# An fp32 encoder block on one core: attention output with V stationary, gate chunks in quarters, conv taps one by one

## The chip, the core and the metric

One core of a Trainium2 chip. The metric is device time in microseconds of one execution of the whole kernel: the lower the better. Engines: TensorE (PE; its weight loads are PEld), VectorE (DVE), ScalarE (ACT), GpSimd (POOL), and the queue of SyncE (SP), which issues the loads.

## The reference, cut to what matters

One layer on 512 tokens of width 1024, all in fp32: a gated feed-forward, a mixer, a second feed-forward and a gated embedding. The mixer projects the normalised input `u` with `w_in` and runs two branches, an attention (MLA) and an mLSTM; the change lies in the attention part of it.

```python
c_q, c_kv, k_r, ml_q, ml_k, ml_v, ml_i, ml_f, ml_o, gates = jnp.split(u @ w_in, split_idx, axis=-1)
# attention: 8 heads, 64 + 32 features per head in q and k, 64 in v, 512 keys
s = einsum('bqhd,bkhd->bhqk', qn, k_nope) + einsum('bqhd,bkd->bhqk', qr, k_rope)
o = einsum('bhqk,bkhd->bqhd', softmax(s * scale, axis=-1), v)
# mLSTM: q, k = silu(depthwise_conv(ml_q | ml_k)), 5 taps; 2 directions, 4 chunks of 128
a, bm = mla_branch(...) @ w_branch_mla, mlstm_branch(...) @ w_branch_ml
mixed = (sigmoid(g_a) * a + sigmoid(g_b) * bm) @ w_out
```

## The kernel before, in words

Products with large weights run as three fp32r matmuls of 512 columns (`three`, L282 to L284, for features on partitions; `three_tm`, L289 to L291, for tokens on partitions): both operands are split into a high and a low part. Weights come in 512 KB chunks through a ring of four: SP loads `w_raw`, ScalarE writes `w_hi` (L305), VectorE `w_lo` (L312), TensorE uses both. `hi_upto` and `lo_upto` place these splits in the programs of ScalarE and VectorE; `GAC`, `MV`, `MO`, `GBC` number the chunks of the first gates, of `ml_v`, of `ml_o` and of the second gates. The attention and the mLSTM cores run as plain fp32 matmuls. Each engine's order is written out by hand in `mixer_pe`, `mixer_dve`, `mixer_act`, `mixer_pool`, with semaphores between them; there is no planner. `B[0]` to `B[7]` are the eight PSUM banks.

Attention goes by heads and by blocks of 128 queries, 32 blocks in all. For each block TensorE makes the scores (L884, Q stationary, 512 keys as columns, banks 2 to 4), VectorE the maximum and the bias (L1142, L1143), ScalarE the exp with its sum (L1345, into `Pm`); one head later TensorE transposes the block of P in four pieces (L892, banks 5 and 6), ScalarE (even blocks, L1348) and VectorE (odd, L1152) copy it to `PT`, and TensorE multiplies (`pv`, L870): the transposed P stationary, 64 columns of V moving, four matmuls per block into bank 7. `o_out` (L1125) scales a head's output with the reciprocal of the sums into `O`, tokens on partitions. Between heads TensorE does one whole chunk of the gates `g_a` (`fm_pair`, banks 0 and 1), and VectorE a `w_lo` split and, for heads 1 to 4, the five conv taps of one tile (`conv_tile`, L1058, L1060). `ga_out` (L1133) empties the gate banks after each second chunk. After the last head `O` is transposed in 16 pieces (L910) and split into `oT_hi` (L1353) and `oT_lo` (L1161). Then come `MV` (V of the mLSTM, L1364), `MO` (`og`, L1387) and the eight units of the mLSTM, the first of which starts with `mb(0)` (L963, L968, banks 2 and 7).

Of the kernel before, what the change touches and what calls it, by code (L numbers as in the profile page):

```python
# [22 lines left out]
ALU = mybir.AluOpType  # L23
ACT = mybir.ActivationFunctionType
# [93 lines left out]
def block_build(nc, w, const, out, ctx):  # L118
# [57 lines left out]
    O = ar("O", [P, TB, S], 64.5)  # L176
    PT = ar("PT", [P, 2, S], 72.5)
# [4 lines left out]
    oT_hi = ar("oT_hi", [P, 4, S], 16.5, F32R)  # L182
    oT_lo = ar("oT_lo", [P, 4, S], 24.5, F32R)
# [612 lines left out]

    def q_padded(hh, c):

        return (mqk if hh % 2 == 0 else tbuf)[:, hh // 2, c * P:(c + 1) * P]

    def mixer_pe(pe):
# [62 lines left out]
        def pv(t):  # L864
            hh, b = t // 4, t % 4
            pe.wait_ge(ms["pt_even"] if t % 2 == 0 else ms["pt_odd"], t // 2 + 1)
            if b == 0 and hh >= 1:
                pe.wait_ge(ms["o_done"], hh)
            for kb in range(TB):
                last = nc.tensor.matmul(B[7][:, b * VDIM:(b + 1) * VDIM], PT[:, t % 2, kb * P:(kb + 1) * P],  # L870
                                        Vm[:, kb, hh * VDIM:(hh + 1) * VDIM], start=(kb == 0), stop=(kb == TB - 1))
            last.then_inc(ms["pv"], 1)

        for hd in range(HEADS + 1):
            for b in range(TB):
                if hd < HEADS:
                    s = 4 * hd + b
                    if b == 0:
                        pe.wait_ge(ms["K_done"], hd + 1)
                    if s < 3:  # L880
                        pe.wait_ge(ms["Vm_done"], s + 2)
                    else:
                        pe.wait_ge(ms["exp"], s - 2)
                    nc.tensor.matmul(B[2 + s % 3][:], Q[:, hd, b * P:(b + 1) * P], K[:, hd, :], start=True,  # L884
                                     stop=True).then_inc(ms["scores"], 1)
                if hd >= 1:
                    t = 4 * (hd - 1) + b
                    pe.wait_ge(ms["exp"], t + 1)
                    if t >= 2:
                        pe.wait_ge(ms["pt_even"] if t % 2 == 0 else ms["pt_odd"], t // 2)  # L890
                    for kb in range(TB):
                        last = nc.tensor.transpose(B[5 + t % 2][:, kb * P:(kb + 1) * P],  # L892
                                                   Pm[:, b, kb * P:(kb + 1) * P], ident[:])
                    last.then_inc(ms["pT"], 1)
                    if t >= 1:
                        pv(t - 1)
            if hd < HEADS:
                if hd % 2 == 0 and hd >= 2:
                    pe.wait_ge(ms["ga"], hd)
                fm_pair(pe, GAC + hd, hd % 2, [0, 1], v_hi, v_lo, KD)  # L900
        pv(4 * HEADS - 1)

        MVB, MOB = [2, 3, 4, 7], [0, 1, 5, 6]
        for j in range(4):
            if j == 0:
                pe.wait_ge(ms["o_done"], HEADS)
            if j >= 2:
                pe.wait_ge(ms["oT_split"], j - 1)
            for tb in range(TB):
                last = nc.tensor.transpose(B[5 + j % 2][:, tb * P:(tb + 1) * P], O[:, tb, j * P:(j + 1) * P], ident[:])  # L910
            last.then_inc(ms["oTT"], 1)
# [27 lines left out]
        for pr in range(2):  # L939
            for c in range(TB):  # L940
                last = nc.tensor.transpose(B[4 + 3 * pr][:, c * P:(c + 1) * P], mqk[:, 2 + pr, c * P:(c + 1) * P], ident[:])
            last.then_inc(ms["kT_T"], 1)
# [29 lines left out]
        pe.wait_ge(ms["q_split"], 6)  # L972
        mb(0)
# [76 lines left out]
    def conv_tile(dve, ct):  # L1050

        o = mqk[:, ct, :]
        wc = VEC["ml_conv_w"]
        for j in range(CONV):
            sc = cols[:, wc + 4 * j + ct:wc + 4 * j + ct + 1]
            src = conv_in[:, ct, j:j + S]
            if j == 0:
                ins = nc.vector.tensor_scalar(o, src, sc, None, ALU.mult)  # L1058
            else:
                ins = nc.vector.scalar_tensor_tensor(o, src, sc, o, ALU.mult, ALU.add)  # L1060
            if j < CONV - 1:
                dlink(dve, ins)
            else:
                ins.then_inc(ms["conv_done"], 1)
# [4 lines left out]
    def mixer_dve(dve):  # L1069
# [51 lines left out]
        def o_out(hh):  # L1121
            dve.wait_ge(ms["exp"], 4 * hh + 4)
            dlink(dve, nc.vector.reciprocal(rsum, sums[:, 4 * hh:4 * hh + 4]))
            dve.wait_ge(ms["pv"], 4 * hh + 4)
            nc.vector.tensor_tensor(O[:, :, hh * VDIM:(hh + 1) * VDIM],  # L1125
                                    B[7][:, 0:4 * VDIM].rearrange("p (b v) -> p b v", b=4),
                                    rsum[:, :, None].broadcast_to([P, TB, VDIM]), ALU.mult).then_inc(ms["o_done"], 1)
            dve.wait_ge(ms["o_done"], hh + 1)

# [5 lines left out]
        for hd in range(HEADS + 1):  # L1135
            for b in range(TB):
                if hd < HEADS:
                    s = 4 * hd + b
                    dve.wait_ge(ms["scores"], s + 1)
                    if s >= 4:  # L1140
                        dve.wait_ge(ms["exp"], s - 3)
                    dlink(dve, nc.vector.tensor_reduce(mx[:, b:b + 1], B[2 + s % 3][:], AX.X, ALU.max))  # L1142
                    nc.vector.tensor_scalar(nb[:, b:b + 1], mx[:, b:b + 1], rqs[:, b:b + 1], -1.0, ALU.mult,  # L1143
                                            ALU.mult).then_inc(ms["nb"], 1)
                if hd >= 2 and b == 0:
                    o_out(hd - 2)
                if hd % 2 == 0 and hd >= 2 and b == 1:
                    ga_out(hd // 2 - 1)
                if hd >= 1 and b % 2 == 1:
                    t = 4 * (hd - 1) + b  # L1150
                    dve.wait_ge(ms["pT"], t + 1)
                    nc.vector.tensor_copy(PT[:, 1, :], B[6][:]).then_inc(ms["pt_odd"], 1)  # L1152
            if hd < HEADS:
                lo_upto(dve, GAC + hd + 3)
                if 1 <= hd <= 4:
                    conv_tile(dve, hd - 1)
        o_out(HEADS - 1)

        for j in range(4):
            dve.wait_ge(ms["oT_hi"], j + 1)  # L1160
            nc.vector.tensor_tensor(oT_lo[:, j, :], B[5 + j % 2][:], oT_hi[:, j, :].bitcast(F32),  # L1161
                                    ALU.subtract).then_inc(ms["oT_split"], 1)
# [152 lines left out]
    def mixer_act(act):  # L1315
# [21 lines left out]
        for hd in range(HEADS + 1):  # L1337
            for b in range(TB):
                t = 4 * (hd - 1) + b
                if hd >= 1:  # L1340
                    act.wait_ge(ms["pT"], t + 1)
                if hd < HEADS:
                    s = 4 * hd + b
                    act.wait_ge(ms["nb"], s + 1)
                    nc.scalar.activation(Pm[:, b, :], B[2 + s % 3][:], ACT.Exp, bias=nb[:, b:b + 1],  # L1345
                                         scale=rqs[:, b:b + 1], accum_out=sums[:, s:s + 1]).then_inc(ms["exp"], 1)
                if hd >= 1 and b % 2 == 0:
                    nc.scalar.activation(PT[:, 0, :], B[5][:], ACT.Copy).then_inc(ms["pt_even"], 1)  # L1348
            if hd < HEADS:
                hi_upto(act, GAC + hd + 3)  # L1350
        for j in range(4):
            act.wait_ge(ms["oTT"], j + 1)
            nc.scalar.activation(oT_hi[:, j, :], B[5 + j % 2][:], ACT.Copy).then_inc(ms["oT_hi"], 1)  # L1353
# [4 lines left out]
        for ct in range(4):  # L1358
            act.wait_ge(ms["conv_done"], ct + 1)
            nc.scalar.activation(mqk[:, ct, :], mqk[:, ct, :], ACT.Silu,  # L1360
                                 bias=col("ml_conv_b", ct)).then_inc(ms["mqk_done"], 1)
        act_after(act, MV + 3)
        for tb in range(TB):
            nc.scalar.activation(V[:, tb, :], B[[2, 3, 4, 7][tb]][:], ACT.Copy, scale=rc[:, tb:tb + 1]).then_inc(ms["Vml"], 1)  # L1364
# [10 lines left out]
        for pr in range(2):  # L1375
            act.wait_ge(ms["kT_T"], pr + 1)
            nc.scalar.activation(K_tm[:, :, pr * P:(pr + 1) * P], v4(B[4 + 3 * pr][:]), ACT.Copy).then_inc(ms["K_tm"], 1)
# [8 lines left out]
        for tb in range(TB):  # L1386
            nc.scalar.activation(og[:, tb, :], B[[0, 1, 5, 6][tb]][:], ACT.Copy,  # L1387
                                 scale=rc[:, tb:tb + 1]).then_inc(ms["mo"], 1)
# [477 lines left out]
```

## Time and profile before

| | us |
|---|---|
| median of 3 runs (1317.93 to 1319.42) | 1318.46 |
| profiled execution | 1314.45 |
| its span, first to last instruction | 1312.5 |
| PE busy | 1253.6 (96%) |
| PEld busy | 1033.7 (79%) |
| DVE busy | 677.8 (52%) |
| ACT busy | 425.5 (32%) |
| POOL busy | 119.0 (9%) |

Busy is the time in which at least one instruction of the engine ran. Matmuls are pipelined, so that records overlap: what a matmul costs in a row of others is read from start to start. A plain fp32 matmul stands in the trace as two records. The mean granted clock of TensorE over the span is 0.979 of 2.4 GHz.

### The profile page before, as it was taken

Reading aid. Unit: us, or ns where it says so; the run is one execution under the profiler, and the core shown is the slowest. Engines: PE = TensorE matmul, PEld = TensorE weight load, DVE = VectorE, ACT = ScalarE, POOL = GpSimd, SP = SyncE. Lnnn points to the kernel's source line nnn. Section 1 sums busy time; section 2 is a strip of 40 time slices with the busy share of each in tenths; the row PEclk is TensorE's granted clock in tenths of the full one; section 3 lists DMA queues with packets and bytes.
Section 4 is the critical chain, followed back from the end, with each engine's and each line's share of the span. In section 5 each row is a group of like instructions: output and inputs, shape, how many; then the busy total and the mean of one; then the engine's idle time right before and its main releaser. Section 6 shows DMA issues by size and latency. Waiting matters only on the chain.

```text
span 1312.5 us, 15620 instructions
## 1 busy us (share of the span) xinstructions
PE 1253.6 (96%) x5909; PEld 1033.7 (79%) x5909; DVE 677.8 (52%) x1042; ACT 425.5 (32%) x612; POOL 119.0 (9%) x96
## 2 busy tenths in 40 slices
PE   5899999999997999999999999989999999999996
PEld 4688888888876877777788878778888888888785
DVE  5744444432237766754555566485444444222774
ACT  3423333221133433335321333243323232112552
POOL 3000000000024000000200200230000000000343
PEclk8899999999998999999999999989999999999997
DMA  5233333222231231110221122213333332333101
GB/s 188 82 111 96 96 96 96 96 97 96 96 74 31 66 112 48 49 32 17 81 88 42 49 80 97 81 48 113 96 96 96 96 96 96 96 98 111 57 24 64
DMA packets 95810, 107.75 MB, mean 82 GB/s; under 512 B 15030, under 2 KB 85398, under 8 KB 95766
## 3 DMA queue, kind: packets, MB, share of 16 engines
q1 hardware_dynamic: 95766, 107.15, 26.3%
q8 instruction: 29, 0.48, 0.1%
q14 instruction: 15, 0.12, 0.0%
HBM read 105.04 MB, written 2.10 MB: 82 GB/s over the span
## 4 chain that ended last, share of the span: by engine, by line
PE 81%; DVE 9%; issue 5%; ACT 2%; POOL 2%; DMA 1%; SPq 0%; DVEq 0%; POOLq 0%; ACTq 0%
PE bank L282 23%; PE bank L284 23%; PE bank L283 23%; PE bank L870 2%; PE bank L884 2%; DVE v_lo L455 1%; PE bank L410 1%; DVE w_lo L312 1%; DVE tbuf L448 1%; PE bank L892 1%; PE bank L289 1%; PE bank L376 1%; POOL sqacc L396 1%; PE bank L290 1%; PE bank L291 1%
## 5 line engine op out<-in xcount | busy, mean ns | idle before, releaser
L312 DVE TENSOR_TENSOR w_lo<-w_raw,w_hi 128x1024 fp32r<-128x1024 f32 x195 | 241.5, 1244 | 386.9 <-ACT w_hi L305 379.5
L282 PE MATMUL bank<-v_hi,w_hi 128*128 128x512 f32 x968 | 381.4, 394 | 6.6 <-DVE w_lo L312 6.2
L284 PE MATMUL bank<-v_hi,w_lo 128*128 128x512 f32 x968 | 377.6, 390 | 0.0
L283 PE MATMUL bank<-v_lo,w_hi 128*128 128x512 f32 x968 | 377.3, 390 | 0.0
L305 ACT ACTIVATE w_hi<-w_raw 128x1024 fp32r<-128x1024 f32 x195 | 203.8, 1054 | 364.5 <-PE bank L284 361.0
L282 PEld LDWEIGHTS bank<-v_hi,w_hi 128*128 128x128 f32 x968 | 182.2, 188 | 44.6 <-DVE w_lo L312 6.5
L284 PEld LDWEIGHTS bank<-v_hi,w_lo 128*128 128x128 f32 x968 | 182.0, 188 | 38.3
L283 PEld LDWEIGHTS bank<-v_lo,w_hi 128*128 128x128 f32 x968 | 182.3, 188 | 37.7 <-issue 0.2
L284 PE MATMUL bank<-prod_hi,w_lo 128*128 (+1 forms) x352 | 137.0, 389 | 0.0
L282 PE MATMUL bank<-prod_hi,w_hi 128*128 (+1 forms) x352 | 137.0, 389 | 0.0
L283 PE MATMUL bank<-prod_lo,w_hi 128*128 (+1 forms) x352 | 137.0, 389 | 0.0
L282 PEld LDWEIGHTS bank<-prod_hi,w_hi 128*128 128x128 f32 x352 | 66.1, 188 | 13.8
L283 PEld LDWEIGHTS bank<-prod_lo,w_hi 128*128 128x128 f32 x352 | 66.1, 188 | 13.7
L284 PEld LDWEIGHTS bank<-prod_hi,w_lo 128*128 128x128 f32 x352 | 66.1, 188 | 13.7
L393 POOL COPY sqacc<-scratch 128x512 f32<-128x512 f32 x4 | 2.4, 611 | 745.8 <-ACT scratch L437 745.8
L675 ACT ACTIVATE prod_hi<-scratch 128x512 f32 (+1 forms) x44 | 27.1, 633 | 110.9 <-DVE scratch L639 110.9
L639 DVE TENSOR_TENSOR scratch<-bank,scratch 128x512 f32<-128x512 f32 x44 | 28.3, 685 | 65.6 <-PE bank L284 65.6
L486 POOL TENSOR_TENSOR sqacc<-sqacc,scratch 128x512 f32<-128x512 f32 x28 | 45.3, 1618 | 24.1 <-ACT scratch L476 24.0
L1345 ACT ACTIVATE Pm<-bank,small 128x512 f32<-128x512 f32 x32 | 24.9, 778 | 64.1 <-DVE small L1143 64.1
L669 ACT ACTIVATE scratch<-scratch 128x512 f32<-128x512 f32 x44 | 27.1, 633 | 53.6 <-DVE scratch L627 53.6
L504 PE MATMUL bank<-v_hi,w_hi 128*128 128x512 f32 x64 | 28.2, 440 | 12.0 <-ACT v_hi L473 12.0
L473 ACT ACTIVATE v_hi<-h,cols 128x512 fp32r<-128x512 f32 x32 | 23.1, 722 | 48.7 <-DVE h L449 44.3
(268 smaller groups left out, 1416.7 us busy)
## 6 DMA issues: line engine op xcount, KB each, us to landing
w_raw<-in_ffn_w_gate SPq DMA_DIRECT2D x44, 512.0 KB, 3.5
w_raw<-in_ffn_w_up SPq DMA_DIRECT2D x44, 512.0 KB, 3.5
w_raw<-in_ffn_w_down SPq DMA_DIRECT2D x44, 512.0 KB, 3.4
w_raw<-in_w_in SPq DMA_DIRECT2D x32, 512.0 KB, 3.6
w_raw<-in_w_out SPq DMA_DIRECT2D x8, 512.0 KB, 3.3
w_raw<-in_ple_w_gate SPq DMA_DIRECT2D x8, 512.0 KB, 3.3
x_tm<-in_x SPq DMA_DIRECT2D x2, 1024.0 KB, 5.1
w_raw<-in_w_branch_mla SPq DMA_DIRECT2D x4, 512.0 KB, 3.3
```

Of the source, the lines that this page charges most:

```text
L282: nc.tensor.matmul(o, whi, a_hi, start=start, stop=False)
L283: nc.tensor.matmul(o, whi, a_lo, start=False, stop=False)
L284: return nc.tensor.matmul(o, wlo, a_hi, start=False, stop=stop)
L305: nc.scalar.activation(w_hi[:, s, :], w_raw[:, s, :], ACT.Copy).then_inc(w_hi_done, 1)
L312: nc.vector.tensor_tensor(w_lo[:, s, :], w_raw[:, s, :], w_hi[:, s, :].bitcast(F32), ALU.subtract).then_inc(w_lo_done, 1)
L486: nc.gpsimd.tensor_tensor(sqacc[:], sqacc[:], scratch[:, m % 4, :], ALU.add).then_inc(b["h_acc"], 1)
L504: nc.tensor.matmul(o[:], whi, v_hi[:, k, :], start=(k == 0), stop=False)
L639: nc.vector.tensor_tensor(scratch[:, 2 + f, :], B[(6 if first else 2) + f][:], scratch[:, f, :], ALU.mult).then_inc(prod_done, 1)
L669: nc.scalar.activation(scratch[:, f, :], scratch[:, f, :], ACT.Silu).then_inc(silu0 if first else silu_done, 1)
L675: nc.scalar.activation(o, scratch[:, 2 + f, :], ACT.Copy).then_inc(phi, 1)
L870: last = nc.tensor.matmul(B[7][:, b * VDIM:(b + 1) * VDIM], PT[:, t % 2, kb * P:(kb + 1) * P], Vm[:, kb, hh * VDIM:(hh + 1) * VDIM], start ...
L884: nc.tensor.matmul(B[2 + s % 3][:], Q[:, hd, b * P:(b + 1) * P], K[:, hd, :], start=True, stop=True).then_inc(ms["scores"], 1)
```

## The change

- The output of attention is made with V stationary (128 keys x 64 features of one head) and the transposed P moving (512 queries). Head 2p goes to partitions 0 to 63 of bank 7, head 2p + 1 to 64 to 127, in turn over the four blocks of keys (`pair_output`). The result has features on partitions: `O`, its transposes and `o_out` are gone; `oT_high` and `oT_low` split bank 7 directly.
- P is scaled by the reciprocal of its sum before it is transposed: a reciprocal of one column on VectorE and one scaling pass on ScalarE per block.
- The blocks go in turn over the two heads of a pair (`head_block`). The transposed P of even blocks (head 2p) is kept in `scratch`, that of odd blocks in `PT_odd`, a whole head each.
- TensorE's steps: `scores(s)`, `p_transposes(s - 4)`, a quarter of a gate chunk (`fm_quarter`, 6 fp32r matmuls); after steps 11, 19, 27 and 35 a `pair_output`. VectorE does one conv tap per step (`conv_tap`, steps 6 to 25).
- Banks: `MV` and `MO` get others, and `mb(0)` waits for the first `og` copy, which reads bank 7. `oT_hi` and `oT_lo` lie interleaved in one tile.

The diff, cut to its core:

```diff
...
+    PT_odd = ar("PT_odd", [P, TB, S], 64.5)
...
+    oT = ar("oT", [P, 4, 2, S], 16.5, F32R)
+    oT_hi, oT_lo = oT[:, :, 0, :], oT[:, :, 1, :]
...
+    def fm_quarter(n, half, banks, kk):
+
+        for f in range(2):
+            k, c = 4 * half + kk, kk * 256 + f * P
+            last = three(B[banks[f]][:], wv(n, c, c + P), v_hi[:, k, :], v_lo[:, k, :], k == 0, k == KD - 1)
+        return last
...
+        def scores(s):
+            hd, b = head_block(s)
+            if b == 0:
+                pe.wait_ge(ms["K_done"], hd + 1)
+            if s < 3:
+                pe.wait_ge(ms["Vm_done"], s + 2)
+            else:
+                pe.wait_ge(ms["exp"], s - 2)
+            nc.tensor.matmul(B[2 + s % 3][:], Q[:, hd, b * P:(b + 1) * P], K[:, hd, :], start=True,
+                             stop=True).then_inc(ms["scores"], 1)
+        def p_transposes(t):
+            pe.wait_ge(ms["norm"], t + 1)
+            if t >= 2:
+                pe.wait_ge(ms["pt_even"] if t % 2 == 0 else ms["pt_odd"], t // 2)
             for kb in range(TB):
+                last = nc.tensor.transpose(B[5 + t % 2][:, kb * P:(kb + 1) * P],
+                                           Pm[:, t % 4, kb * P:(kb + 1) * P], ident[:])
+            last.then_inc(ms["pT"], 1)
+        def pair_output(pr):
+            pe.wait_ge(ms["pt_even"], 4 * pr + 4)
+            pe.wait_ge(ms["pt_odd"], 4 * pr + 4)
+            if pr >= 1:
+                pe.wait_ge(ms["oT_split"], pr)
+            for kb in range(TB):
+                for e in range(2):
+                    hd = 2 * pr + e
+                    last = nc.tensor.matmul(B[7][64 * e:64 * e + 64, :], Vm[:, kb, hd * VDIM:(hd + 1) * VDIM],
+                                            (scratch if e == 0 else PT_odd)[:, kb, :], start=(kb == 0),
+                                            stop=(kb == TB - 1))
             last.then_inc(ms["pv"], 1)
 
+        for s in range(STEPS + 4):
+            if s < STEPS:
+                scores(s)
+            if s >= 4:
+                p_transposes(s - 4)
+                c, kk = (s - 4) // 4, s % 4
+                if kk == 0:
+                    pe.wait_ge(w_lo_done, GAC + c + 1)
+                    if c % 2 == 0 and c >= 2:
+                        pe.wait_ge(ms["ga"], c)
+                last = fm_quarter(GAC + c, c % 2, [0, 1], kk)
+                if kk == 3:
+                    last.then_inc(w_used, 1)
+            if s >= 11 and s % 8 == 3:
+                pair_output(s // 8 - 1)
+        MVB, MOB = [5, 2, 3, 4], [7, 0, 1, 6]
...
-                last = nc.tensor.transpose(B[4 + 3 * pr][:, c * P:(c + 1) * P], mqk[:, 2 + pr, c * P:(c + 1) * P], ident[:])
+                last = nc.tensor.transpose(B[4 + pr][:, c * P:(c + 1) * P], mqk[:, 2 + pr, c * P:(c + 1) * P], ident[:])
...
+        pe.wait_ge(ms["mo"], 1)
         mb(0)
...
+    def conv_tap(dve, i):
+        ct, j = i // CONV, i % CONV
         o = mqk[:, ct, :]
+        c = VEC["ml_conv_w"] + 4 * j + ct
+        src = conv_in[:, ct, j:j + S]
+        if j == 0:
+            ins = nc.vector.tensor_scalar(o, src, cols[:, c:c + 1], None, ALU.mult)
+        else:
+            dve.wait_ge(ms["conv_tap"], i)
+            ins = nc.vector.scalar_tensor_tensor(o, src, cols[:, c:c + 1], o, ALU.mult, ALU.add)
+        ins.then_inc(ms["conv_tap"], 1)
+    STEPS = HEADS * TB
+    def head_block(s):
+        return 2 * (s // 8) + s % 2, s % 8 // 2
...
+        def oT_low(pr):
+            dve.wait_ge(ms["oT_hi"], pr + 1)
+            nc.vector.tensor_tensor(oT_lo[:, pr, :], B[7][:], oT_hi[:, pr, :].bitcast(F32),
                                     ALU.subtract).then_inc(ms["oT_split"], 1)
+        for s in range(STEPS + 4):
+            if s < STEPS:
+                b, q = head_block(s)[1], s % 4
+                dve.wait_ge(ms["scores"], s + 1)
+                if s >= 4:
+                    dve.wait_ge(ms["exp"], s - 3)
+                dlink(dve, nc.vector.tensor_reduce(mx[:, q:q + 1], B[2 + s % 3][:], AX.X, ALU.max))
+                nc.vector.tensor_scalar(nb[:, q:q + 1], mx[:, q:q + 1], rqs[:, b:b + 1], -1.0, ALU.mult,
+                                        ALU.mult).then_inc(ms["nb"], 1)
+            if 2 <= s < STEPS + 2:
+                r = s - 2
+                dve.wait_ge(ms["exp"], r + 1)
+                if r >= 4:
+                    dve.wait_ge(ms["norm"], r - 3)
+                nc.vector.reciprocal(rsum[:, r % 4:r % 4 + 1], sums[:, r:r + 1]).then_inc(ms["rsum"], 1)
+            if s in (12, 20, 28):
+                ga_out(s // 8 - 1)
+            if s >= 14 and s % 8 == 6:
+                oT_low(s // 8 - 1)
+            if s >= 4 and s % 2 == 1:
+                t = s - 4
+                dve.wait_ge(ms["pT"], t + 1)
+                nc.vector.tensor_copy(PT_odd[:, :, head_block(t)[1] * P:(head_block(t)[1] + 1) * P],
+                                      v4(B[6][:])).then_inc(ms["pt_odd"], 1)
+            if s % 4 == 1 and s >= 5:
+                lo_upto(dve, GAC + (s - 5) // 4 + 3)
+            if s >= 6 and s - 6 < 4 * CONV:
+                conv_tap(dve, s - 6)
+        ga_out(3)
+        oT_low(3)
...
+        def oT_high(pr):
+            act.wait_ge(ms["pv"], pr + 1)
+            nc.scalar.activation(oT_hi[:, pr, :], B[7][:], ACT.Copy).then_inc(ms["oT_hi"], 1)
+        for s in range(STEPS + 4):
+            t = s - 4
+            if t >= 0:
+                act.wait_ge(ms["pT"], t + 1)
+            if s < STEPS:
+                b, q = head_block(s)[1], s % 4
+                act.wait_ge(ms["nb"], s + 1)
+                nc.scalar.activation(Pm[:, q, :], B[2 + s % 3][:], ACT.Exp, bias=nb[:, q:q + 1],
+                                     scale=rqs[:, b:b + 1], accum_out=sums[:, s:s + 1]).then_inc(ms["exp"], 1)
+            if t >= 0 and t % 2 == 0:
+                bt = head_block(t)[1]
+                nc.scalar.activation(scratch[:, :, bt * P:(bt + 1) * P], v4(B[5][:]), ACT.Copy).then_inc(ms["pt_even"], 1)
+            if 2 <= s < STEPS + 2:
+                q = (s - 2) % 4
+                act.wait_ge(ms["rsum"], s - 1)
+                act.wait_ge(ms["exp"], s - 1)
+                nc.scalar.activation(Pm[:, q, :], Pm[:, q, :], ACT.Copy, scale=rsum[:, q:q + 1]).then_inc(ms["norm"], 1)
+            if s >= 14 and s % 8 == 6:
+                oT_high(s // 8 - 1)
+            if s % 4 == 0 and s >= 4:
+                hi_upto(act, GAC + (s - 4) // 4 + 3)
+        oT_high(3)
...
-            act.wait_ge(ms["conv_done"], ct + 1)
+            act.wait_ge(ms["conv_tap"], CONV * (ct + 1))
...
+            nc.scalar.activation(V[:, tb, :], B[[5, 2, 3, 4][tb]][:], ...
+            nc.scalar.activation(K_tm[...], v4(B[4 + pr][:]), ...
+            nc.scalar.activation(og[:, tb, :], B[[7, 0, 1, 6][tb]][:], ...
```

## Rows read from the trace of the kernel before

**Rows 1.** The page, part 4: the chain that ended last, by engine.

```profile
PE 81%; DVE 9%; issue 5%; ACT 2%; POOL 2%; DMA 1%; SPq 0%; DVEq 0%; POOLq 0%; ACTq 0%
```

**Rows 2.** Busy time of the attention stretch (columns: PE, PEld, DVE, ACT, POOL, PEclk, DMA share, GB/s).

```profile
487.86:611.12 123.26, 119.49 (x656) 91.38 (x655) 72.97 (x135) 46.49 (x93) 0.00 (x0) 1.00 0.13 39
```

**Rows 3.** Timeline of one head's steps (start us, duration us, engine, line, operation).

```profile
541.02 0.39 PE L284 MATMUL bank<-v_hi,w_lo 128*128 128x512 f32 x1
...
541.25 1.02 PE L884 MATMUL bank<-K,Q 128*128 128x512 f32 x2
...
542.11 0.60 PE L892 MATMUL bank<-ident,Pm 128*128 128x128 f32 x4
...
542.54 1.00 PE L870 MATMUL bank<-Vm,PT 128*128 128x64 f32 x8
...
543.38 1.08 PE L884 MATMUL bank<-K,Q 128*128 128x512 f32 x2
...
550.55 0.48 PE L282 MATMUL bank<-v_hi,w_hi 128*128 128x512 f32 x1
550.63 0.19 PEld L283 LDWEIGHTS bank<-v_lo,w_hi 128*128 128x128 f32 x1
550.87 0.39 PE L283 MATMUL bank<-v_lo,w_hi 128*128 128x512 f32 x1
```

**Rows 4.** Groups by line, 487.8 to 611.1 us: attention output on TensorE.

```profile
L870 PE MATMUL bank<-Vm,PT 128*128 128x64 f32 x256 | 34.1, 276 | 1.7 <-ACT PT L1348 0.7 <-DVE PT L1152 0.3 <-DVE O L1125 0.2
```

**Rows 5.** Timeline of TensorE at the end of the stretch.

```profile
599.74 0.39 PE L284 MATMUL bank<-v_hi,w_lo 128*128 128x512 f32 x1
...
607.95 1.09 PE L910 MATMUL bank<-ident,O 128*128 128x128 f32 x8 [0.59 <-DVE O L1125]
610.14 1.25 PE L910 MATMUL bank<-ident,O 128*128 128x128 f32 x8 [1.10 <-DVE oT_lo L1161]
611.15 0.47 PE L289 MATMUL bank<-w_hi,v_hi 128*128 128x512 f32 x1
```

**Rows 6.** Timeline of TensorE at the start of the stretch.

```profile
487.86 2.74 PE L884 MATMUL bank<-K,Q 128*128 128x512 f32 x6
490.98 1.12 PE L884 MATMUL bank<-K,Q 128*128 128x512 f32 x2 [0.39 <-ACT Pm L1345]
491.55 0.80 PE L282 MATMUL bank<-v_hi,w_hi 128*128 128x512 f32 x1
```

**Rows 7.** Groups by line, same stretch: VectorE and ScalarE (`Vm`: 476 to 490 us).

```profile
L1345 ACT ACTIVATE Pm<-bank,small 128x512 f32<-128x512 f32 x32 | 24.9, 778 | 64.1 <-DVE small L1143 64.1
L1142 DVE TENSOR_REDUCE small<-bank 128x1 f32<-128x512 f32 x32 | 22.1, 690 | 27.7 <-PE bank L884 27.2
...
L1060 DVE SCALAR_TENSOR_TENSOR mqk<-conv_in,cols,mqk 128x512 f32<-128x512 f32 x16 | 12.0, 752 | 0.6
...
L312 DVE TENSOR_TENSOR w_lo<-w_raw,w_hi 128x1024 fp32r<-128x1024 f32 x9 | 11.0, 1224 | 10.2 <-ACT w_hi L305 10.2
...
L1348 ACT ACTIVATE PT<-bank 128x512 f32<-128x512 f32 x16 | 9.4, 588 | 7.0 <-PE bank L892 7.0
...
L1143 DVE TENSOR_SCALAR small<-small 128x1 f32<-128x1 f32 x32 | 6.8, 214 | 1.1
...
L1133 DVE TENSOR_TENSOR gates_a<-bank,r_b 128x512 f32<-128x512 f32 x8 | 5.1, 681 | 0.0
...
L1123 DVE RECIPROCAL small<-small 128x4 f32<-128x4 f32 x8 | 1.3, 168 | 0.0
...
L1335 ACT ACTIVATE Vm<-bank,small 128x512 f32<-128x512 f32 x4 | 2.8, 688 | 2.8 <-PE bank L291 2.8
```

**Rows 8.** Timeline around the first `Mb` group, 655 to 664 us.

```profile
658.90 1.15 PE L963 MATMUL bank<-Mrows,ident 8*128 8x128 f32 x8
659.01 2.42 ACT L1387 ACTIVATE og<-bank,small 128x512 f32<-128x512 f32 x4 [1.93 <-PE bank L291]
...
661.48 0.50 PE L282 MATMUL bank<-v_hi,w_hi 128*128 128x512 f32 x1 [0.34 <-ACT og L1387]
```

More of the change, by code:

```diff
@@ L175, in block_build @@
     Pm = ar("Pm", [P, TB, S], 56.5)
-    O = ar("O", [P, TB, S], 64.5)
-    PT = ar("PT", [P, 2, S], 72.5)
+    PT_odd = ar("PT_odd", [P, TB, S], 64.5)
     mqk = ar("mqk", [P, 4, S], 76.5)
@@ L180, in block_build @@
     i_row = tbuf[0:8, 1, :]
-    oT_hi = ar("oT_hi", [P, 4, S], 16.5, F32R)
-    oT_lo = ar("oT_lo", [P, 4, S], 24.5, F32R)
+    oT = ar("oT", [P, 4, 2, S], 16.5, F32R)
+    oT_hi, oT_lo = oT[:, :, 0, :], oT[:, :, 1, :]
     gates_b = ar("gates_b", [P, 8, S], 32.5)
@@ L862, in mixer_pe @@
         pe.wait_ge(ms["Q_done"], HEADS)
[L864 to L868, printed above, removed]
-            for kb in range(TB):
-                last = nc.tensor.matmul(B[7][:, b * VDIM:(b + 1) * VDIM], PT[:, t % 2, kb * P:(kb + 1) * P],
-                                        Vm[:, kb, hh * VDIM:(hh + 1) * VDIM], start=(kb == 0), stop=(kb == TB - 1))
-            last.then_inc(ms["pv"], 1)
@@ L874, in mixer_pe @@
[L874 to L911, printed above, removed]
+        def scores(s):
[8 more added lines that the diff above has]
+                             stop=True).then_inc(ms["scores"], 1)
@@ L1048, in block_build @@
     UNITS = [(0, 0), (1, 3), (0, 1), (1, 2), (0, 2), (1, 1), (0, 3), (1, 0)]
-    def conv_tile(dve, ct):
+    def conv_tap(dve, i):
+        ct, j = i // CONV, i % CONV
         o = mqk[:, ct, :]
[L1053 to L1064, printed above, removed]
+        c = VEC["ml_conv_w"] + 4 * j + ct
[9 more added lines that the diff above has]
+        return 2 * (s // 8) + s % 2, s % 8 // 2
     def v4(ap):
@@ L1119, in mixer_dve @@
                                     ALU.mult).then_inc(ms["K_done"], 1)
[L1121 to L1128, printed above, removed]
         def ga_out(g):
@@ L1133, in ga_out @@
                 nc.vector.tensor_tensor(gates_a[:, 2 * g + f, :], B[f][:], r_b[:], ALU.mult).then_inc(ms["ga"], 1)
[L1135 to L1161, printed above, removed]
-                                    ALU.subtract).then_inc(ms["oT_split"], 1)
+        def oT_low(pr):
+            dve.wait_ge(ms["oT_hi"], pr + 1)
+            nc.vector.tensor_tensor(oT_lo[:, pr, :], B[7][:], oT_hi[:, pr, :].bitcast(F32),
+                                    ALU.subtract).then_inc(ms["oT_split"], 1)
@@ L1335, in mixer_act @@
             nc.scalar.activation(Vm[:, tb, :], B[VB[tb]][:], ACT.Copy, scale=rq[:, 4 + tb:5 + tb]).then_inc(ms["Vm_done"], 1)
[L1337 to L1353, printed above, removed]
+        def oT_high(pr):
[23 more added lines that the diff above has]
+        oT_high(3)
         for m in range(8):
@@ L1363, in mixer_act @@
         for tb in range(TB):
-            nc.scalar.activation(V[:, tb, :], B[[2, 3, 4, 7][tb]][:], ACT.Copy, scale=rc[:, tb:tb + 1]).then_inc(ms["Vml"], 1)
+            nc.scalar.activation(V[:, tb, :], B[[5, 2, 3, 4][tb]][:], ACT.Copy, scale=rc[:, tb:tb + 1]).then_inc(ms["Vml"], 1)
         for d in range(2):
@@ L1376, in mixer_act @@
             act.wait_ge(ms["kT_T"], pr + 1)
-            nc.scalar.activation(K_tm[:, :, pr * P:(pr + 1) * P], v4(B[4 + 3 * pr][:]), ACT.Copy).then_inc(ms["K_tm"], 1)
+            nc.scalar.activation(K_tm[:, :, pr * P:(pr + 1) * P], v4(B[4 + pr][:]), ACT.Copy).then_inc(ms["K_tm"], 1)
         act.wait_ge(ms["decb_ps"], 1)
@@ L1386, in mixer_act @@
         for tb in range(TB):
-            nc.scalar.activation(og[:, tb, :], B[[0, 1, 5, 6][tb]][:], ACT.Copy,
+            nc.scalar.activation(og[:, tb, :], B[[7, 0, 1, 6][tb]][:], ACT.Copy,
                                  scale=rc[:, tb:tb + 1]).then_inc(ms["mo"], 1)
```

## The prediction, made before the changed kernel ran

> **What bounds the kernel now.** I read the chain of waits first: 81% of the span is TensorE, 9% VectorE [rows 1]. Then the stretch that the change rewrites, from the first score matmul to the first matmul of the `MV` chunks, 487.86 to 611.15 us, 123.3 us: TensorE is busy for 119.5 us of it at a full granted clock (1.00) [rows 2]. So the stretch is worth what TensorE issues in it, plus the waits that its order makes. The timeline of one head gives the price of each kind of group, from start to start [rows 3]: after a gate matmul (541.02, next 541.25) the score matmul takes 0.86 us (541.25 to 542.11, two records, since a plain fp32 matmul is recorded as two passes), the four transposes of a block 0.43, the four attention-output matmuls of a block 0.84 (542.54 to 543.38, eight records of 64 columns). In the gate matmuls (fp32r, 512 columns) one start follows another after 0.23 us, the first after fp32 work after 0.32 (550.55 to 550.87). Attention output has 256 records in all, the largest group after the gates: 34.1 us busy [rows 4]. Last, the end of the stretch: the last gate matmul starts at 599.74, `MV` at 611.15; in these 11.4 us stand a head of output, 16 transposes of `O` and two waits for VectorE (0.59 and 1.10 us) that nothing covers [rows 5].
>
> **The change part by part.** TensorE's own work in the new order:
>
> Scores: 32 x 0.86 = 27.5 us. Transposes of P: 32 x 0.43 = 13.8 us. Both as before.
>
> Gate quarters: 32 groups of 6 fp32r matmuls. A group costs 0.32 + 5 x 0.23 = 1.46 us, since each now follows fp32 transposes: 46.6 us. Before, 8 groups of 24 cost 8 x (0.32 + 23 x 0.23) = 44.9; the cutting costs 1.7 us.
>
> Attention output: 32 matmuls of 512 columns in place of 128 of 64. One is 2 records of 0.43 us, as the score matmul, of the same columns and type [rows 3], so a pair of heads is 16 records. Here the trace of before shows no operation of the kind: nothing in it fills only half of the columns. Bounds: if the two halves never run side by side, 16 x 0.43 = 6.9 us a pair, 27.5 in all, about what the 256 short records take; if they always do, 3.4 us a pair, 13.8 in all. Below that it can't fall, each half having 8 records to stream. I take nearly full overlap. The two heads write different partitions of the bank and hold separate weights, but the order of issue is e0, e0, e1, e1: with starts in order, the first record of e1 can only go with the second of e0, so the pair takes one record more than the bound, 9 x 0.43 = 3.9 us, 15.5 us in all. The row nearest to it is the score matmul's, which can't choose between the ends: it gives the price of a record, not which records share time. I choose the overlap because each stream reads 512 columns in 0.43 us, so two at once read no faster than one fp32r stream does now (512 in 0.23 us): no rate is asked for that the trace does not show. Both ends stay in the range.
>
> The `O` transposes, their waits and the rounds through ScalarE and VectorE between them (607.95 to 611.15 [rows 5]) go. In their place `oT` is split out of bank 7 while TensorE goes on with other work: three of four in the middle of the steps; the last is needed only by `MO`, behind 96 matmuls of `MV`, 96 x 0.23 = 22 us. What is late next there is nothing.
>
> Sum of work: 27.5 + 13.8 + 46.6 + 15.5 = 103.4 us.
>
> Waits in the new order, on TensorE:
>
> 1. Gate banks 0 and 1. At steps 12, 20 and 28 the first quarter of a new pair waits for both of `ga_out`, which VectorE now issues in the same step, behind max, `nb` and reciprocal of that step's scores. VectorE needs 0.69 + 0.21 + 0.17 + 2 x 0.68 us from the end of the scores [rows 7], somewhat less where short ones follow closely, say 2.3 with the handing over; TensorE has 0.43 us of transposes to do meanwhile, and the end of a score record lies 0.17 us behind the next start. 2.1 us each, three times: 6.4. Everything behind it in TensorE's queue waits too, and so the next scores. Before, `ga_out` stood two blocks ahead of its use and no such wait shows. For this wait the bounds are 1.5 and 2.8 us.
>
> 2. The start. Before, the gates of head 0 (from 491.55) cover the first exp. Now steps 0 to 3 have only scores: the wait for exp before the fourth stays, and the first transposes must wait for exp, reciprocal and the scaling of P, about 0.5 us more; 1.1 in all [rows 6].
>
> 3. `pair_output` waits for the odd copy of its own step. The copy comes after VectorE has done the step's max, `nb` and reciprocal, and whatever it is behind; a quarter (1.46 us) covers most. I take 0.1, 1.0 and 0.4 us for pairs 0 to 2, nothing for the last.
>
> 4. VectorE and ScalarE per step. VectorE in steps 6 to 25: 1.07 for max, `nb`, reciprocal; 0.75 conv tap; a copy every second step 0.34 (0.68 like the passes of `ga_out`, which have its size); `w_lo` 1.22 every fourth 0.31; `ga_out` and `oT_low` every eighth 0.26 [rows 7]: 2.7 us. TensorE's step is 0.86 + 0.43 + 1.46 = 2.75, and with its share of `pair_output` 3.2. ScalarE: exp 0.78 + 0.19, scaling 0.69 (as the copy with a scale of `Vm`; from SBUF it is not shown, bounds 0.6 to 0.8), copy of every second block 0.29, `w_hi` and `oT_high` about 0.35: 2.3 us. Both fit on average, but VectorE with little room, and bunched in the steps after `ga_out`; scaled blocks then come late for the transposes. 2.5 us in all. Bounds 0 and 8.
>
> Waits together 6.4 + 1.1 + 1.5 + 2.5 = 11.5 us. The stretch: 103.4 + 11.5 = 114.9 us, against 123.3: 8.4 us less.
>
> After it one wait is new: the first `Mb`/`QK` group waits for the copy of `og` out of bank 7. ScalarE starts it at 659.01; it takes 0.69, so the group starts at 659.75 in place of 658.90 and ends some 2.1 us later, at 661.9 (8 records that take 1.15 us by the row, and 16 of the same 128 columns); the gates behind it waited anyway for the fourth `og` copy, until 661.48 [rows 8]. Cost 0.4 us. The other bank numbers and the place of `oT` move nothing. No DMA is added, and the weight queue keeps its distance: gate chunk c (from 3 on) is split in step 4c - 7 and used from step 4c + 4.
>
> Result: -8.4 + 0.4 = -8.0 us. The profiled execution took 1314.45 us around a span of 1312.5; the median of the timed runs is 1318.46. The difference is of the work, so it is applied to the median: 1310.5 us (span 1304.5).
>
> A rule to weigh: weight loads of 0.19 us lie under a running matmul now (550.63 under the one from 550.55 [rows 3]). The Trainium skill (TensorE: Matmul & The Clock Gate, Part 3) says that a load overlaps matmuls in flight only where the row groups differ, and both heads here use all rows. By that rule each of a half's records would have its load in front; by the row it is free. For the full array the trace contradicts the rule. The same page has matmuls in different column groups run at the same time and gives 2.38 times for three of them, which is what the forecast needs; no run here shows it yet.
>
> **The rivals.**
>
> (a) The halves do not run side by side: 16 x 0.43 = 6.9 us a pair, 12.0 us more in all. Everything else stands, so the new order loses: -8.0 + 12.0 = +4.0 us, 1322.5 us, slower. For it: every record of TensorE in the trace starts after the one before has streamed. Against it: there each uses all columns. It decides from 5.9 us a pair on, where the gain is nil. This is also the case in which the change doesn't do what it says.
>
> (b) The halves overlap, but VectorE paces the steps: each instruction there has its own wait now, since conv taps no longer run as a block. With 0.1 us more for each of some five a step, VectorE's step is 3.2 us and with bunching passes TensorE's; 20 steps by 0.2 to 0.3 are 5 us: 1315.5 us. For it: 2.7 of 3.2 us already. Against it: VectorE's short instructions follow one another closely now.
>
> (c) The loads of a half are not hidden. A load of 64 columns is half of 0.19 us, so a pair takes 9 x 0.53 = 4.8 us, 3.4 us more in all: 1314 us. The skill's rule quoted above would do this. The trace of before speaks against it, for the full array.
>
> **How the numbers follow.** Forecast 0.47, (a) 0.28, (b) 0.17, (c) 0.08. The forecast's own range is 1306 to 1315 (waits 7 to 16 us, pairs 3.4 to 4.3). 0.2% is 2.6 us, about what can be told from no change. Faster by more than that (below 1315.8): the forecast, half of (b), most of (c): 0.63. Slower (above 1321.1): two thirds of (a) with some mishaps: 0.22. Within: 0.15. The range for 8 in 10 takes in (a): 1305 to 1323.5.
>
> **What would show it.** In the changed profile: attention output as 64 records with 128x64 weights; by their starts, 3.9 or 6.9 us between the last quarter and the next scores at steps 11, 19, 27 and 35. Three waits of some 2 us of a gate matmul for `gates_a`. `MV` starting 114.9 us after the first score. No transposes of `O`. Waits of the transposes for the scaled P over 3 us in sum would speak for (b). It is wrong if a pair takes over 5.9 us, or if the granted clock falls in the stretch, which nothing in the trace of before announces.

## The result, and the profile after

The changed kernel takes 1307.64 us (median of 4 runs, 1304.88 to 1308.09) against 1318.2 before (4 runs): ratio 0.9924, 95% interval 0.9908 to 0.9939. It is 10.6 us faster; the forecast was 8.0. Run again beside the experiments it took 1307.63 against 1317.1, ratio 0.9925 (0.9911 to 0.994). The profiled execution took 1308.09 us, with a span of 1306.3.

The page and the attention stretch of the changed kernel, first score matmul to first `MV` matmul; the columns are those of [rows 1, 2]:

```profile
PE 79%; DVE 9%; issue 6%; ACT 3%; POOL 2%; DMA 1%; SPq 0%; DVEq 0%; ACTq 0%; POOLq 0%
```

```profile
489.52:602.60 113.08, 104.37 (x449) 65.76 (x447) 68.86 (x152) 65.08 (x125) 0.00 (x0) 0.98 0.14 43
```

The stretch went from 123.3 to 113.1 us: 10.2 us, about the measured gain. TensorE's busy time fell by 15 us, from 119.5 to 104.4, and its idle time rose from 3.8 to 8.7 us, so a third of what its work lost came back as waits. The granted clock is 0.98 in the stretch, where it was 1.00 [rows 2]. The spans of the two profiled executions differ by only 6.2 us (1312.5 and 1306.3): that of the kernel before ran 4 us under its median, and the changed one has 6.8 us at 1.2 GHz around 444 to 452 us and 3.4 us around 652 to 657, outside the stretch, which the trace of before does not have.

One step, the first pair of heads and the step after it, on TensorE (to be held against [rows 3]; the columns are start us, duration us, engine, line, operation, with the idle time before it and what ended it in brackets):

```profile
499.36 1.02 PE L878 MATMUL bank<-K,Q 128*128 128x512 f32 x2
500.21 0.60 PE L886 MATMUL bank<-ident,Pm 128*128 128x128 f32 x4
500.57 0.47 PE L281 MATMUL bank<-v_hi,w_hi 128*128 128x512 f32 x1
...
502.04 1.02 PE L878 MATMUL bank<-K,Q 128*128 128x512 f32 x2
...
515.88 0.61 PE L899 MATMUL bank<-scratch,Vm 128*64 128x512 f32 x1 [0.24 <-DVE PT_odd L1166]
515.88 0.64 PE L899 MATMUL bank<-PT_odd,Vm 128*64 128x512 f32 x1
516.33 0.59 PE L899 MATMUL bank<-scratch,Vm 128*64 128x512 f32 x1
516.36 0.59 PE L899 MATMUL bank<-PT_odd,Vm 128*64 128x512 f32 x1
...
518.90 0.59 PE L899 MATMUL bank<-scratch,Vm 128*64 128x512 f32 x1
518.94 0.59 PE L899 MATMUL bank<-PT_odd,Vm 128*64 128x512 f32 x1
519.46 1.12 PE L878 MATMUL bank<-K,Q 128*128 128x512 f32 x2
520.42 0.60 PE L886 MATMUL bank<-ident,Pm 128*128 128x128 f32 x4
522.96 0.47 PE L281 MATMUL bank<-v_hi,w_hi 128*128 128x512 f32 x1 [1.94 <-DVE gates_a L1137]
```

The weights are now 128x64, and each record of `scratch` (head 2p) has one of `PT_odd` (head 2p + 1) 0.00 to 0.04 us behind it: the halves run side by side. A pair takes 3.58 us (515.88 to 519.46). Each keeps the pace of a full-width record, 0.43 us. A step without waits is 2.68 us (499.36 to 502.04).

The wait for `gates_a` counts for more than its 1.94 us: from the transposes to the gate matmul behind it pass 2.54 us (520.42 to 522.96) in place of 0.36 (500.21 to 500.57), so each of the three delays the queue by 2.18 us.

What TensorE waited for in the stretch (total us, times, longest):

```profile
PE bank L281 <- DVE gates_a L1137: 5.8, 3, 1.9
PE bank L899 <- ACT scratch L1363: 1.7, 2, 1.2
PE bank L886 <- ACT Pm L1368: 0.6, 2, 0.4
PE bank L878 <- ACT Pm L1359: 0.4, 1, 0.4
PE bank L899 <- DVE PT_odd L1166: 0.2, 1, 0.2
```

The list puts two of the three waits of `pair_output` to ScalarE's copy into `scratch`. The rows say otherwise; for the second pair:

```profile
539.71 1.23 DVE L311 TENSOR_TENSOR w_lo<-w_raw,w_hi 128x1024 fp32r<-128x1024 f32 x1 [1.07 <-ACT w_hi L304]
...
543.31 0.59 ACT L1363 ACTIVATE scratch<-bank 128x512 f32<-128x512 f32 x1
...
544.00 0.67 DVE L1166 COPY PT_odd<-bank 128x512 f32<-128x512 f32 x1
...
544.78 0.61 PE L899 MATMUL bank<-scratch,Vm 128*64 128x512 f32 x1 [1.22 <-ACT scratch L1363]
```

ScalarE's copy was done at 543.90, VectorE's odd copy at 544.67, 0.11 us before the matmul. So it is at 572.76 too (odd copy done at 572.65, scratch copy at 572.54). VectorE was late there, and it had stood 1.07 us waiting for ScalarE's `w_hi` in the step before.

The end of the stretch (against [rows 5]) and the new wait behind it (against [rows 8]):

```profile
597.09 0.60 PE L886 MATMUL bank<-ident,Pm 128*128 128x128 f32 x4
599.02 0.64 PE L899 MATMUL bank<-scratch,Vm 128*64 128x512 f32 x1
...
602.60 0.50 PE L288 MATMUL bank<-w_hi,v_hi 128*128 128x512 f32 x1
```

```profile
650.85 1.12 PE L972 MATMUL bank<-Mrows,ident 8*128 8x128 f32 x8 [0.87 <-ACT og L1407]
```

No transposes of `O`, no wait before `MV`; `Mb` waits 0.87 us for `og`.

### The profile page after: what moved, and what is told of

It is laid out like the page before. It is cut to its first block, busy times and chain, and to the rows that moved or that the text cites. A ratio compares the mean times of both kernels' runs of the same rounds, so it can differ in the third digit from the quotient of the medians.

```text
span 1306.3 us, 15298 instructions
## 1 busy us (share of the span) xinstructions
PE 1243.8 (95%) x5701; PEld 1012.9 (78%) x5701; DVE 671.8 (51%) x1058; ACT 443.9 (34%) x644; POOL 118.8 (9%) x96
## 4 chain that ended last, share of the span: by engine, by line
PE 79%; DVE 9%; issue 6%; ACT 3%; POOL 2%; DMA 1%; SPq 0%; DVEq 0%; ACTq 0%; POOLq 0%
PE bank L281 23%; PE bank L283 23%; PE bank L282 23%; DVE v_lo L454 1%; PE bank L899 1%; PE bank L409 1%; PE bank L878 1%; DVE w_lo L311 1%; DVE small L1150 1%; DVE tbuf L447 1%; PE bank L375 1%; PE bank L288 1%; POOL sqacc L395 1%; PE bank L290 1%; PE bank L289 1%
```

## The experiments

All edits are to the changed kernel; ratios are to the kernel before. "Stretch" is read in each trace, first score to `MV`, and PEclk is the granted clock in it as a share of 2.4 GHz. The runs came in three groups, each beside its own runs of the kernel before: the changed kernel again, e3, e6 and e7 (before: 1317.1 us), e1, e2, e4 and e5 (1318.12 us), e8, e9 and e7 again (1316.36 us). Between groups the ratios and the stretches compare, the medians only to about 1 us.

| | us, median | ratio (95%) | stretch | PEclk in it |
|---|---|---|---|---|
| changed, again | 1307.63 | 0.9925 (0.9911 to 0.9940) | 116.3 | 0.96 |
| e1 heads grouped | 1312.3 | 0.9948 (0.9930 to 0.9966) | 121.2 | 0.97 |
| e2 heads one after the other | 1322.71 | 1.0034 (1.0023 to 1.0045) | 131.0 | 0.96 |
| e3 `ga_out` early | 1299.66 | 0.9866 (0.9851 to 0.9881) | 105.0 | 1.00 |
| e4 whole gate chunks | 1311.69 | 0.9952 (0.9935 to 0.9968) | 118.3 | 0.99 |
| e5 conv in blocks | 1317.26 | 0.9992 (0.9979 to 1.0004) | 122.2 | 0.97 |
| e6 old banks | 1305.95 | 0.9923 (0.9907 to 0.9939) | 112.4 | 0.98 |
| e7 = e3 + e6 | 1297.43 | 0.9847 (0.9834 to 0.9861) | 105.0 | 1.00 |
| e7, again | 1297.83 | 0.9854 (0.9837 to 0.9870) | 104.9 | 1.00 |
| e8 = e7, pair later | 1295.91 | 0.9840 (0.9826 to 0.9853) | 103.1 | 1.00 |
| e9 P not scaled | 1303.32 | 0.9894 (0.9878 to 0.9910) | 109.8 | 0.98 |

**The changed kernel again.** No edit. Expected:

> The changed kernel again, beside the experiments on the same chip. The trace of its first profiled execution has 113.1 us from the first score matmul to MV against 123.3 before, so 10 us less than before are expected, 1307.5 to 1308.5. If part of the 10.6 us first measured was luck of the clock outside the stretch, it comes out nearer 1310.

The gain repeats (9.5 us). The stretch is 3.2 us longer than in the first trace, with the same waits to 0.1 us; the clock is the difference. The gates after the first wait for `gates_a`, in this trace:

```profile
521.58 0.64 PE L281 MATMUL bank<-v_hi,w_hi 128*128 128x512 f32 x1 [1.94 <-DVE gates_a L1137]
522.01 0.63 PE L282 MATMUL bank<-v_lo,w_hi 128*128 128x512 f32 x1
522.44 0.63 PE L283 MATMUL bank<-v_hi,w_lo 128*128 128x512 f32 x1
522.87 0.63 PE L281 MATMUL bank<-v_hi,w_hi 128*128 128x512 f32 x1
```

They start 0.43 us apart in place of 0.23: the lower of the two levels, 1.2 GHz, for 3.4 us, after which the step is normal. Such a fall of the clock comes after each of the three waits in this trace and after one in the first; 3.2 us for two more falls makes 1.6 us each.

**e2: one head after the other.**

```diff
-            for kb in range(TB):
-                for e in range(2):
+            for e in range(2):
+                if e == 1:
+                    last.then_inc(ms["pv_first"], 1)
+                    pe.wait_ge(ms["pv_first"], pr + 1)
+                for kb in range(TB):
```

> pair_output does the four matmuls of the first head, waits for them, and then those of the second: the halves cannot run side by side. Theory (the gain is the overlap of the halves): a pair takes 6.9 us plus a handing over of 0.2 us in place of 3.6, so 13 to 14 us more than the changed kernel, 1321, slower than before by 2 to 4 us. Rival (the gain came from the removed tail and the filled steps): at most 5 us more than the changed kernel.

```profile
514.53 3.62 PE L902 MATMUL bank<-scratch,Vm 128*64 128x512 f32 x8 [0.24 <-DVE PT_odd L1169]
518.20 3.65 PE L902 MATMUL bank<-PT_odd,Vm 128*64 128x512 f32 x8
521.78 1.12 PE L878 MATMUL bank<-K,Q 128*128 128x512 f32 x2
```

A pair takes 7.25 us (514.53 to 521.78), 3.66 more than with overlap, and the stretch grows by 14.7 us = 4 x 3.66. The kernel is slower than before (1.0034). The overlap is worth more than the whole gain; all else in the change, as it was built, loses. The cost came out a little above the theory, 14.7 us for 13 to 14. The rest need not lose: the best version below (e8) gains 20.5 us, of which 14.7 are the overlap, so some 6 us come from the rest by this estimate.

**e1: heads grouped, no wait.**

```diff
-            for kb in range(TB):
-                for e in range(2):
+            for e in range(2):
+                for kb in range(TB):
```

> As changed, but the four matmuls of the first head are issued before the four of the second, with no wait between. Theory A (records start in the order of issue): only the last record of one head and the first of the other share time, 6.5 us a pair, 11 to 12 us more than the changed kernel. Theory B (each half of the columns has a line of its own, and a waiting record does not hold up those of the other half): 3.6 us a pair, no difference.

```profile
513.48 2.33 PE L899 MATMUL bank<-scratch,Vm 128*64 128x512 f32 x5 [0.24 <-DVE PT_odd L1166]
515.22 0.64 PE L899 MATMUL bank<-PT_odd,Vm 128*64 128x512 f32 x1
515.65 0.59 PE L899 MATMUL bank<-scratch,Vm 128*64 128x512 f32 x1
515.70 0.59 PE L899 MATMUL bank<-PT_odd,Vm 128*64 128x512 f32 x1
...
516.56 2.31 PE L899 MATMUL bank<-PT_odd,Vm 128*64 128x512 f32 x5
518.80 1.12 PE L878 MATMUL bank<-K,Q 128*128 128x512 f32 x2
```

Neither A (6.5) nor B (3.6): 5.32 us a pair. Head 2p + 1 starts with the fifth record of head 2p, while three more of that head stand ahead of it in the program. So in this trace records of the other half pass those that wait for their own, but only a few; what sets how many was not tried. All four pairs are alike (5.32 to 5.35 us). The time moved by 3 to 5 us, as one goes by the ratios or the medians, against 7 from four pairs. In the traces it closes: 4 x 1.74 = 7.0 us for the pairs, 0.3 less of waits at `pair_output` and one fall of the clock less (1.6) make 5.1, and the stretch is 4.9 us longer.

**e3: `ga_out` early.**

```diff
-            if s in (12, 20, 28):
-                ga_out(s // 8 - 1)
...
                 conv_tap(dve, s - 6)
+            if s in (11, 19, 27):
+                ga_out(s // 8 - 1)
```

> ga_out moved from steps 12, 20, 28 to the end of steps 11, 19, 27 on VectorE, where it runs under pair_output. Theory (the gate banks are emptied too late): the three waits of 1.94 us of the gate matmuls for gates_a go, and nothing comes in their place: 5.5 to 6 us less than the changed kernel, up to 7.5 if the stretches at half clock that follow such a wait go too. Rival (VectorE paces the steps, the wait only shows where it is collected): the waits come back at the transposes or at pair_output, less than 2 us gained.

VectorE empties the banks from 516.17 on, under `pair_output` (516.01), and the gates run on at 520.91. The waits left in its stretch:

```profile
PE bank L899 <- ACT scratch L1363: 1.7, 2, 1.2
PE bank L886 <- ACT Pm L1368: 0.6, 2, 0.4
PE bank L878 <- ACT Pm L1359: 0.4, 1, 0.4
PE bank L899 <- DVE PT_odd L1164: 0.2, 1, 0.2
```

The line of `gates_a` is gone, the others are unchanged to the digit, and the clock is 1.00. The kernel gains 8.0 us, a little over the upper end. In the traces the stretch shrinks by three delays of 2.18 us, 6.5 in all, and by 1.6 us for each fall of the clock that went: with one in the first trace of the changed kernel that is 8.1 us (113.1 to 105.0), with three in the second 11.3 us (116.3 to 105.0). The rival falls: VectorE does not pace the steps.

**e6: the old banks.** `MV` in banks 2, 3, 4, 7 and `MO` in 0, 1, 5, 6, the K transposes in 4 and 7, and

```diff
+                    if n0 == MV and k == 0 and tb == 3:
+                        pe.wait_ge(ms["oT_split"], 4)
...
-        pe.wait_ge(ms["mo"], 1)
         mb(0)
```

> The banks of MV, MO and the K transposes as before the change, so mb(0) waits for no og copy; MV waits for bank 7 at its fourth token block. Theory: the wait of 0.87 us for og before Mb goes, the gates behind it still wait for the fourth og copy, so 0.4 to 0.6 us less than the changed kernel, and no wait for oT at MV, since nine matmuls (2 us) stand before it against 1.4 us for splitting bank 7. Rival: MV waits 0.5 us or more for bank 7, and nothing is gained.

In the trace the wait for `og` before `Mb` is gone and `MV` does not wait. The time alone can't tell (0.9923 against 0.9925). On top of e3 the medians differ by 2.2 us (e7), but from the last `MO` matmul to the first of the gates behind `Mb` the traces have 3.23 us in e3 and 2.90 in e7, only 0.33 less. The clock may be part of the rest: with the `og` wait it falls right behind it in five of eight traces (1.6 us each), with the old banks in none.

**e7: both.**

> The edits of e3_ga_early and e6_old_banks together. If they are independent, 6 to 7 us less than the changed kernel, 1301 to 1302. If VectorE paces the steps, 1306 or more.

> e7_ga_and_banks again, beside e8_pair_late on the same chip: 1297.5 us as before, within 0.2%.

10.2 us less than the changed kernel, and the same time again in another group. That is 3 us more than was expected: e3 had been put at 5.5 to 6 us and brought 8.0, e6 at 0.4 to 0.6 and brought 1.7 by the medians. Neither edit undoes the other (8.0 and 1.7 us alone), and 1306 or more, the other case, is excluded.

**e8: `pair_output` after the next scores** (steps 12, 20, 28 and the end), with e7.

```diff
             if s < STEPS:
                 scores(s)
+            if s in (12, 20, 28):
+                pair_output(s // 8 - 1)
...
-            if s >= 11 and s % 8 == 3:
-                pair_output(s // 8 - 1)
+        pair_output(3)
```

> The two edits of e7_ga_and_banks, and pair_output(0) to (2) after the scores of the next step, so that 0.86 us of other work stands before it. Theory (the waits of pair_output for the copies of scratch and PT_odd, 1.9 us in the trace of e7, are only a matter of place): 1.5 to 2 us less than e7_ga_and_banks, 1295.5 to 1296. Rival (ScalarE is late on average, so the wait moves to the transposes): no difference.

1.9 us less than e7 in the same group, 104.9 to 103.1 in the stretch, as the theory had it. Its waits:

```profile
PE bank L886 <- ACT Pm L1370: 0.6, 2, 0.4
PE bank L878 <- ACT Pm L1361: 0.4, 1, 0.4
PE bank L899 <- issue: 0.4, 1, 0.4
```

This is the best version: 1295.91 us, 0.984 (0.9826 to 0.9853) of the kernel before.

**e9: P not scaled.** The pass `Pm <- Pm * rsum` on ScalarE is left out, and its waits go to the exp.

> The changed kernel without the scaling pass of P on ScalarE (the attention output stays unnormalised), all waits on it taken to the exp instead. If ScalarE paces the steps, the 2.3 us of waits for scratch and for scaled P go, and with the lead VectorE gains some of the waits for gates_a too: 2 to 4 us less than the changed kernel. If not, only those 2.3 us or less.

4.3 us less by the medians (4.1 by the ratios), over the upper end of the first case. The trace speaks for the second: the 5.8 us for `gates_a` stay whole, and the waits for `scratch`, `PT_odd` and scaled P (2.5 us) are gone. Against the first trace of the changed kernel, which has one fall of the clock in the stretch as this one has, the stretch is 3.3 us shorter, 2.5 of waits and 0.8 of slower starts beside them; the rest of the 4.3 is not accounted for. ScalarE does not pace the steps, but its pass is what makes the copies late: VectorE's wait for `w_hi` in the step before the second pair, 1.07 us with the pass, is 0.29 without it, and `pair_output` then waits for nothing.

**e4: whole chunks.** The four quarters at `kk == 3`, with the wait for `ga` there.

> Each gate chunk whole after four steps in place of a quarter per step, all else as changed. Theory (quarters give VectorE and ScalarE the time that a block costs them): a step without a quarter is 1.3 us on TensorE against 2.0 to 2.2 on ScalarE, so the transposes wait for scaled P, 4 to 14 us in sum, less the 6 us of gates_a waits and the 1.7 of first-matmul starts that go: from 3 us faster to 6 slower than the changed kernel. Rival (quarters only cost): 6 to 8 us faster.

```profile
PE bank L886 <- ACT Pm L1365: 11.7, 17, 1.1
PE bank L878 <- ACT Pm L1356: 0.4, 1, 0.4
```

4 us more than the changed kernel (0.9952), though no wait for `gates_a` is left: 17 transposes wait 11.7 us for scaled P. Against e3, which is also rid of `gates_a`, the quarters are worth 11 to 12 us.

**e5: conv taps in blocks of five** after steps 9, 13, 17 and 21.

> The five conv taps of a tile as a block after steps 9, 13, 17 and 21 on VectorE, all else as changed. Theory (VectorE has room only if the taps are spread): a block of 3.5 us delays the max of the next scores and the odd copy; the lag is up to 3 us against two steps of slack, so 1 to 5 us more than the changed kernel, at the transposes and at pair_output. Rival (the slack of two steps takes a block up): within 1 us of it.

```profile
PE bank L281 <- DVE gates_a L1137: 5.8, 3, 1.9
PE bank L886 <- ACT Pm L1369: 4.5, 6, 1.2
PE bank L899 <- ACT scratch L1364: 2.8, 1, 2.8
PE bank L899 <- DVE PT_odd L1166: 2.0, 1, 2.0
PE bank L878 <- ACT Pm L1360: 0.4, 1, 0.4
```

9 to 10 us more, twice the upper end, and no faster than before the change. The waits come where the theory had them (15.5 us in sum against 8.7); the size was wrong. Against the first trace of the changed kernel the stretch is 9.1 us longer: 6.8 us of waits, 1.6 for one fall of the clock more, and 0.7 that stays open.

## Why the prediction was right, point by point

1. The overlap of the halves, the step on which it stood, is shown twice: by the pairs of records and by e2, which is rival (a) built, at 7.25 us a pair. The size was a little off: 3.58 us a pair for 3.9, since the order of issue does not hold back the first record of the second head. 4 x 0.3 = 1.2 us. That e2 took 1322.7 us where (a) has 1322.5 is partly luck: its pairs cost more than (a) has (7.25 us for 6.9) and the rest of the stretch less.
2. Quarters and steps: 2.68 us for 2.75. The price of a quarter was right (1.47); transposes between score and gate matmuls take 0.36, not 0.43, which was read where output matmuls follow them. Over 32 blocks that is 2.2 us.
3. The wait for `gates_a`: three delays of 2.18 us for 2.1, by the order of VectorE's instructions, and removable (e3).
4. `pair_output` waits 0.24, 1.22 and 0.46 us, and not at the last pair, where 0.1, 1.0, 0.4 and nothing were forecast, each time for VectorE's odd copy, as forecast. Too high was the last term, 2.5 us for scaled blocks that come late: 0.4 us of waits. Counted from start to start the two terms are 2.7 us for 4.0. Rival (b), VectorE paces the steps, falls with e3; that its slack is small is shown by e5.
5. The start: five score matmuls and 1.0 us of delay stand before the first transposes (489.52 to 494.80), for 1.1.
6. What was missed: the clock. "The granted clock falls in the stretch" was named as what would upset the sum, with nothing in the trace to announce it. It falls, for 3.4 us each time, behind 11 of the 21 waits for `gates_a` in the seven traces that have them, and not at all in the stretch in the four traces without these waits and with quarters. That such waits bring the fall is likely, not shown: in e5 it falls behind waits of 1.96 and 2.81 us at `pair_output` and behind none for `gates_a`, in e4 once where the waits before it are 0.8 and 0.9 us.
7. `Mb` after `og`: it waits 0.87 us, as worked out (0.85), and the gates behind it come 0.33 us later (e3 against e7), for 0.4.
8. Rival (c) falls: a load of 64 columns takes 0.14 us (for the 0.1 put there) and hides. The rule of the Trainium skill (TensorE: Matmul & The Clock Gate, Part 3), that a load overlaps matmuls in flight only where row groups differ, does not hold here: both halves use all rows, and the pace stays 0.43. The same part also lets a load into the background weight buffer go ahead, which would allow this; no run here tells whether that is the way. Its statement that column groups run at the same time does: a pair in 3.58 us against 7.25.

The sum: 114.9 us were forecast for the stretch, and the first trace has 113.1. Counted from start to start, transposes came out 2.2 us under their terms, pairs 1.2, copies and scaled P 1.3. Above them came 1.1 us for the quarters and scores, most of it next to half-width records (the last quarter before a pair takes 1.57 us without a wait, the score behind a pair 0.96), and 1.6 for the clock, which the sum did not have. So the mechanism was right term by term, and that the total came within 2 us is in part that the errors cancel.

## What to carry to other kernels

Two matmuls with 64 output features each can share TensorE if they write different halves of the partitions, but issue them in turn: grouped by head they overlap in part only. Where a buffer is emptied in the same step in which it is needed again, look at what the emptying engine has in front of it and move it under the nearest long piece of the bottleneck's work: that was worth 8 us here, as much as the change had been forecast to bring. When a list of waits names an engine, look at the rows for which operation ended last. Small pieces of filler on every engine (a quarter chunk, one tap) let a pipeline of four steps run; in blocks the same work cost 9 to 12 us.

## What the runs showed of the hardware

- Records for the other half of the columns pass waiting ones, but not all: with eight of one half first, the other half began with the fifth (e1).
- The granted clock fell to 1.2 GHz for 3.4 us behind 11 of 21 waits of 1.94 us on TensorE, and behind five of eight waits of 0.87 us (for `og`). It did not fall in the stretch in e3, e7 (twice) and e8, whose longest waits are 0.4 to 1.3 us. A fall costs 1.6 us here, nearly the wait itself. It is not only waits: in ten of the thirteen traces it also falls at 444 to 452 us, where no wait over 0.15 us stands before it but 32 matmuls of one column do. The cause is open.
- Half-width plain fp32 records keep the pace of full-width ones (0.43 us for 512 columns), alone (e2) and two at a time.
